# Twelve heads' gate products and low parts, moved from VectorE to GpSimd in the two last layers

## The reference

```python
h = rms_norm(x, pre_w)
proj = h @ w_in
...
y_a = diff_attention(qa, ka, va, lam, subln_w, lam_init)     # 4 heads, difference of two softmaxes
...                                                          # 16 heads of 64, window 128, with sinks
y_b = sliding_window_attention(qb, kb, vb, sinks)
...                                                          # 4 heads with low-rank queries and keys
y_c = causal_attention(qc, kc, vc, (MLA_NOPE_DIM + MLA_ROPE_DIM) ** -0.5)
y = jnp.concatenate([y_a, y_b, y_c], axis=-1) * jax.nn.silu(jnp.concatenate([a_g, b_g, c_g], axis=-1))
out = y @ w_out
return x + rms_norm(out, post_w)
```

## Time and profile before

| | |
|---|---|
| median of 3 runs | 3057.1 us (3055.59 to 3057.51) |
| profiled execution | 3059.03 us |
| its span | 3057.3 us |
| granted TensorE clock, mean | 0.993 |
| busy, share of the span: TensorE | 99% |
| VectorE | 70% |
| ScalarE | 48% |
| GpSimd | 10% |
| DMA, share of 16 engines | 50%, 548 MB, 179 GB/s |

### The profile page before, as it was taken

How to read it: one execution, slowest core, us unless ns; L and a number is a source line. 1 busy time by engine, 2 the same in 40 slices (tenths; PEclk the granted TensorE clock), 3 DMA queues, 4 the chain that set the end, 5 groups by cost and what they waited for, 6 DMA issues and landing times. The chain is left out here.

```text
span 3057.3 us, 46940 instructions
## 1 busy us (share of the span) xinstructions
PE 3016.4 (99%) x17446; PEld 2645.2 (87%) x17446; DVE 2153.5 (70%) x2854; ACT 1456.8 (48%) x1821; POOL 290.7 (10%) x191
## 2 busy tenths in 40 slices
PE   8999999999999999999999999999999999999999
PEld 7888888888888888888888888888888888888888
DVE  6776765767666677676856666676788865789764
ACT  5334543434334554555533333344566645656544
POOL 0003300000000400004100000002300004200003
PEclk9999999999999999999999999999999999999999
DMA  6555455555555445444455554555444445444445
GB/s 254 181 190 185 170 184 191 192 187 186 190 192 184 165 174 179 167 177 179 176 184 189 193 188 171 204 192 186 159 165 165 158 145 190 166 167 152 160 146 190
DMA packets 77287, 548.44 MB, mean 179 GB/s; under 512 B 8561, under 2 KB 9073, under 8 KB 11377
## 3 DMA queue, kind: packets, MB, share of 16 engines
q1 hardware_dynamic: 77168, 546.81, 50.0%
HBM read 544.68 MB, written 2.10 MB: 179 GB/s over the span
## 5 line engine op out<-in xcount | busy, mean ns | idle before, releaser
L869 ACT ACTIVATE w_high<-raw 128x2048 fp32r<-128x2048 f32 x511 | 974.3, 1908 | 1149.4 <-DMA raw<-stream 1148.9
L1292 DVE TENSOR_TENSOR w_low<-raw,w_high 128x2048 fp32r<-128x2048 f32 x511 | 1164.9, 2280 | 139.3 <-ACT w_high L869 136.7
L311 PE MATMUL acc<-xs,w_high 128*128 128x512 f32 x4444 | 1094.0, 394 | 0.6 <-ACT w_high L869 0.6
L311 PEld LDWEIGHTS acc<-xs,w_high 128*128 128x128 f32 x4444 | 815.5, 189 | 166.8 <-issue 7.6
L311 PE MATMUL acc<-inner,w_high 128*128 128x512 f32 x2880 | 692.7, 391 | 0.0
L311 PEld LDWEIGHTS acc<-inner,w_high 128*128 128x128 f32 x2880 | 527.9, 188 | 101.6 <-issue 0.7
L318 PEld LDWEIGHTS acc<-xs,w_low 128*128 128x128 f32 x4450 | 578.7, 192 | 21.3
L318 PE MATMUL acc<-xs,w_low 128*128 128x256 f32 x4450 | 593.6, 283 | 0.0
L1301 DVE TENSOR_REDUCE y<-acc 128x256 f32<-128x512 f32 x374 | 258.0, 690 | 433.4 <-PE acc L318 427.6
L318 PEld LDWEIGHTS acc<-inner,w_low 128*128 128x128 f32 x2976 | 382.2, 191 | 15.1
L318 PE MATMUL acc<-inner,w_low 128*128 128x256 f32 x2976 | 386.7, 282 | 0.0
(11 more groups left out here) (184 smaller groups left out, 1585.3 us busy)
## 6 DMA issues: line engine op xcount, KB each, us to landing
raw<-stream SPq DMA_DIRECT2D x514, 1024.0 KB, 4.8
out<-finished SPq DMA_DIRECT2D x8, 256.0 KB, 2.1
h<-x_t SPq DMA_DIRECT2D x3, 512.0 KB, 9.9
raw<-stream SPq DMA_DIRECT2D x2, 512.0 KB, 6.4
consts<-tables SPq DMA_DIRECT2D x1, 960.0 KB, 16.0
h<-x_t SPq DMA_DIRECT2D x2, 256.0 KB, 4.6
branch<-w_spatial SPq DMA_DIRECT2D x1, 512.0 KB, 16.7
branch<-b_spatial SPq DMA_DIRECT2D x1, 512.0 KB, 17.5
```

What stands on the lines that cost most here:

```text
L311: nc.tensor.matmul(acc[s if bank is None else bank][:, :], w_high[:, s, kt * P:(kt + 1) * P], x[:, kt, :, :], start=(kt == first_of[0]), s ...
L869: nc.scalar.activation(w_high[:, s, 0:units * P], raw[:, s, 0:units * P], ACT.Copy)\
L1292: V.tensor_tensor(w_low[:, s, 0:units * P], raw[:, s, 0:units * P], w_high[:, s, 0:units * P], ALU.subtract).then_inc(low_ready, 1)
```

## The change

In both hybrid layers GpSimd multiplies the results of the four differential heads and of the eight window blocks with their gates and makes their low parts. VectorE only brings the result out of PSUM: `halve` multiplies by 0.5 as it copies. For the differential heads the 0.5 goes into the constant `1 - lam_init`. ScalarE still makes the high parts. The four latent heads keep `finish` and `split_low` on VectorE, and `finish` gets two more waits. GpSimd's stream gets `gated(hd, ...)`: for the differential heads each behind its root, for the window blocks one after another, and then the two last roots. Each `gated` waits for the copy (`out_read`), the gate (`gate_ready`) and its own last subtraction, multiplies, waits for ScalarE's high part and subtracts.

```diff
@@ GpSimd, per layer @@
-                for i in range(7):
-                    root(8 + 8 * l + i)
+                r0, o0, split0 = 8 + 8 * l, 16 + 16 * l, 160 + 16 * l
+                root(r0)
+
+                def gated(hd, gate_of):
+
+                    pool.wait_ge(sem("out_read"), o0 + hd + 1)
+                    pool.wait_ge(sem("gate_ready"), 16 * l + hd + 1)
+                    pool.wait_ge(sem("inner_ready"), split0 + hd)
+                    nc.gpsimd.tensor_tensor(source[:, 0, :], normed, gate_of, ALU.mult).then_inc(sem("source_ready"), 1)
+                    pool.wait_ge(sem("inner_high"), split0 + hd + 1)
+                    pool.wait_ge(sem("source_ready"), 144 + 16 * l + hd + 1)
+                    nc.gpsimd.tensor_tensor(inner[:, hd, 1, :], source[:, 0, :], inner[:, hd, 0, :], ALU.subtract)\
+                        .then_inc(sem("inner_ready"), 1)
+                for hd in range(DA_HEADS):
+                    root(r0 + 1 + hd)
+                    gated(hd, diff_gates[hd % 2])
+                for b in range(SW_BLOCKS):
+                    gated(DA_HEADS + b, gate[:, :])
+                for i in range(2):
+                    root(r0 + 5 + i)
@@ VectorE @@
                 def diff_finish(hd):
 
                     scale_out(r0 + 1 + hd, 5 + 7 * l + hd, scale_lat[:, 0, :])
+                    dve.wait_ge(sem("source_ready"), 144 + 16 * l + hd)
                     V.scalar_tensor_tensor(out=normed[:, :], in0=head_out[:, 0:TOKENS], scalar=dyn_col(subln_gain, l),
                                            in1=scale_lat[:, 0, :], op0=ALU.mult, op1=ALU.mult)\
                         .then_inc(sem("out_read"), 1)
-                    dve.wait_ge(sem("out_read"), o0 + hd + 1)
-                    dve.wait_ge(sem("gate_ready"), gate0 + hd + 1)
-                    V.scalar_tensor_tensor(out=source[:, 0, :], in0=normed[:, :], scalar=0.5, in1=diff_gates[hd % 2],
-                                           op0=ALU.mult, op1=ALU.mult).then_inc(sem("source_ready"), 1)
+
+                def halve(o, done):
+
+                    dve.wait_ge(sem("head_done"), done)
+                    dve.wait_ge(sem("source_ready"), 144 + 16 * l + o)
+                    V.tensor_scalar(normed[:, :], head_out[:, 0:TOKENS], 0.5, None, ALU.mult).then_inc(sem("out_read"), 1)
 
                 def finish(o, g, done, gate_of=gate[:, :]):
+
+                    dve.wait_ge(sem("source_ready"), 144 + 16 * l + o)
+                    dve.wait_ge(sem("inner_ready"), split0 + o)
...
-                            finish(DA_HEADS + b - 1, DA_HEADS + b - 1, done0 + DA_HEADS + 2 * b)
+                            halve(DA_HEADS + b - 1, done0 + DA_HEADS + 2 * b)
...
-                        split_low(split0 + DA_HEADS + b - 1, DA_HEADS + b - 1, 0)
...
-                        finish(11, 11, done0 + DA_HEADS + 2 * SW_BLOCKS)
+                        halve(11, done0 + DA_HEADS + 2 * SW_BLOCKS)
...
-                    if i == 1:
-                        split_low(split0 + 11, 11, 0)
@@ host @@
-        col[:, LAM_INIT + LAYERS + layer] = 1 - lam_init
+        col[:, LAM_INIT + LAYERS + layer] = 0.5 * (1 - lam_init)
```

More of the change, by code:

```diff
@@ L1784, in _ @@
                     ahead(c + 1, (s + 1) % 4)
-                    if hd > 1:
-                        split_low(split0 + hd - 2, hd - 2, 0)
                     sum_halves(c + 2, (s + 2) % 4)
@@ L1807, in _ @@
                 ahead(c + 1, 1)
-                split_low(split0 + hd - 1, hd - 1, 0)
                 sum_halves(c + 2, 2)
```

## The result

| | before | after |
|---|---|---|
| median of 17 runs each | 3057.1 us (3054.06 to 3061.63) | 3064.2 us (3060.93 to 3066.36) |
| profiled execution | 3059.03 us | 3064.19 us |
| its span | 3057.3 us | 3062.5 us |

The changed kernel is slower by 7.1 us: ratio 1.0023, 95% interval 1.0016 to 1.0029. The forecast was 3065.5, slower.

The account below looks back on a forecast made before the run. VectorE's order was taken to set the second layer's window passes, and nearly the first's. Per layer 0.50 (first pass) + 3.42 (six full) + 0.27 (last) = 4.2 us, two layers 8.4, on 3057.1 gives 3065.5; range 3059.0 to 3070.5.

Parts of the forecast that it names:

- the wait ahead of `gate_out`: Window passes: VectorE idles before refilling the single gate buffer until GpSimd has multiplied; +0.41 us per full pass.
- the low part colliding behind `w_low`: Window passes: GpSimd's subtraction waits for `w_low`, then holds up VectorE's next small addition; +0.50 us per pass.
- no loss in the other stretches: Differential heads and latent stretch: VectorE's idle time hides the change; zero cost.
- Rival 2: Window passes: VectorE isn't held at `gate_out`, TensorE sets the pace and wins at most 1.0 us; 3056, chance 0.05.
- rival 1: Behind `w_low`: the subtraction hardly disturbs VectorE, 0.15 us instead of 0.50; +3.0 us, 3060, chance 0.22.
- rival 3: Window passes: GpSimd costs more, by fp32r output or two collisions, 1.0 us per subtraction; 3073, chance 0.08.
- The saved subtraction: Window passes: VectorE no longer makes its own low-part subtraction; -0.34 us per pass.
- A full pass: Window passes, six per layer: wait, collision and saved subtraction, +0.41 + 0.50 - 0.34 = +0.57 us each.
- The first pass: First window pass, with the last differential head: wait +0.34, collision +0.50, saved subtraction -0.34, together +0.50 us.
- The last block: Last window pass: probabilities come 0.91 us later against a reserve of 0.69 us; +0.27 us per layer.
- What could be won: Window passes: time taken from VectorE can win about 1 us in the kernel, TensorE's waits for `q_t`.
- One sign: Profile after, window passes: TensorE waits for `q_t` once per pass, 0.5 to 0.6 us.

Follow-up runs that it names:

- early_high: The changed kernel with ScalarE's high part made ahead of the exponentials in every window pass; median +1.1 us against the kernel before, ratio 1.0001.
- late_gate: The changed kernel with `gate_out` moved behind the masks and maxima in the window passes, one gate buffer; median -4.3 us against the kernel before, ratio 0.9985.
- late_and_early: late_gate with ScalarE's high part also made ahead of the exponentials; median -4.4 us against the kernel before, ratio 0.9987.

## Why the prediction was right, and where it was off

- **Direction, place and both mechanisms** held: the wait ahead of `gate_out` in every pass, the low part colliding behind `w_low`, no loss in the other stretches. Rival 2 fell with the 0.85 us of idle VectorE, rival 1 with the 0.71 us addition, rival 3 with GpSimd's own times, 0.74 for the multiply and 0.75 for a subtraction into fp32r that nothing holds (the first pass), and with one collision per pass.
- **The wait**: forecast +0.41 us per pass, from 1.33 us between copy and `gate_out`. Measured 1.27 (2806.79 to 2808.06), +0.35. The multiply was 0.74 as taken from rows 6; the two handovers were 0.11 together, not 0.17.
- **The collision**: forecast +0.50 between 0.40 and 0.56. Measured from the small addition to the reciprocal 0.74 us where it was 0.19, +0.55. The upper bound, 0.56, was nearly right: the blocked operation ended 0.29 us behind GpSimd's with 256 columns, but 0.02 with two.
- **The saved subtraction**, -0.34, was right. A full pass came to +0.56 by these rows against the forecast +0.57. TensorE's passes grew by 0.59 us in the first layer (13.83 to 14.42) and 0.52 in the second (14.01 to 14.53, means of the last four). Six middle passes gave 3.6 and 2.8 us against the forecast 3.42 each; with the estimate of 0.6 us for the profile of the kernel before, the second is 3.4 too.
- **The first pass** was the mis-sized term: forecast +0.50, measured +0.02 (14.28 to 14.30). In it ScalarE makes the high part ahead of the exponentials; `window` says so in its branch `lone`, and I had read rows 8 into all passes. So the subtraction doesn't collide, and the wait (+0.36: 1.41 us from `diff_finish`'s copy at 2749.82 to `gate_out` at 2751.23, 1.05 before) and the saved subtraction (-0.34) are left:

```profile
2751.65 0.75 POOL L1290 TENSOR_TENSOR inner<-source,inner 128x256 fp32r<-128x256 f32 x1 [0.53 <-ACT inner L926]
...
2756.52 0.15 DVE L1482 TENSOR_TENSOR small<-small 128x2 f32<-128x2 f32 x1
```

  The kernel had early_high's order in its own first pass. Seeing it would have taken about 1 us off the forecast and pointed to the remedy.
- **The last block** was off too: forecast +0.27, measured +0.02 from the last scores to the transposes. The transposes wait bank by bank, and the first needs only the first bank's probabilities. The reserve in rows 10 was read to the end of both; the real one is longer by the second bank's work, and all that showed in the pass above is a transpose group of 0.88 instead of 0.82 us.
- These two terms are 0.73 of the 0.93 us per layer between the forecast (4.19) and the mean of 3.64 and 2.88, 1.5 us in the kernel. The forecast of +8.4 less 1.5 is 6.9, near the measured 7.1.
- **What could be won** was mis-sized: at most 1.0 us, read from the table of waits (rival 2 is priced by it). late_gate and late_and_early won 4.3. TensorE's own pass is 13.68 us, and in the first layer, where no wait was shown, their stretch is 1.49 us shorter than before.
- **One sign failed** for the same reason: TensorE was to wait for `q_t` 0.5 to 0.6 us in every pass, and the table shows 0.7 us in four waits in the second layer and 0.2 in one in the first. The time lies in the distances of TensorE's groups. From the first group of the weighing to the scores it is 1.35 us after (2819.04 to 2820.39), 1.13 before (2814.81 to 2815.94) and 0.81 in late_gate (2811.72 to 2812.53).

## What to carry to other kernels

When work goes to another engine, count three things beside its duration there: who must now wait for it in the old engine's order (here a single buffer that is refilled two instructions later), which instructions of the old engine can't run beside the moved work at that moment, and in which pass of a loop the order differs. Here a small addition with two SBUF inputs, behind a long subtraction with two, was where GpSimd got in first, in 14 of 16 passes; masks (one input in PSUM) and maxima (a reduction of one SBUF tensor, 0.61 to 0.62 us) kept their length beside GpSimd, so the moved work belongs there. Moving one line can be worth more than the move of the work: here it turned +7 us into -4, because VectorE had set the pace of the passes before as well.

## What the runs showed of the hardware that I had not expected

The exclusion isn't limited to operations with two SBUF inputs. In late_and_early GpSimd's subtraction meets the small minimum L1472, which reads one SBUF tensor of two columns and a scalar; alone it takes 0.23 us, here 0.65 and, in the next pass, 0.81. It is so in 10 of the 16 passes:

```profile
2797.63 0.65 DVE L1472 TENSOR_SCALAR small<-small 128x2 f32<-128x2 f32 x1 [0.16 <-DVE small L1468]
...
2799.55 0.23 DVE L1472 TENSOR_SCALAR small<-small 128x2 f32<-128x2 f32 x1 [0.16 <-DVE small L1468]
```

GpSimd's subtraction ran from 2797.53 to 2798.26; the minimum ended at 2798.28. In the next pass the minimum is recorded from 2811.31, 0.05 us ahead of the subtraction, and still ends behind it (2812.12 against 2812.09). A mask, with one input in SBUF and one in PSUM, ran beside GpSimd's multiply (2796.16 to 2796.89) at its normal length (from 2796.27, 0.56 us). The Trainium skill (SBUF — State Buffer, section Who interferes with whom) names this case: a `tensor_scalar` from SBUF to SBUF can enter a mode that uses both ports, and then excludes GpSimd. The rows agree with the exclusion; that the minimum runs in such a mode no run shows. Why early_high's minima stayed at 0.23 us is a matter of time: GpSimd's subtraction there ends (2801.70 + 0.75 = 2802.45) before the first of them starts at 2802.80.
